# Prompt attention: scores issued ahead of the subtraction for the block two back, absolute values ahead of the weights

## The chip, the cores and the metric

One core of a Trainium2 chip runs the whole program. The metric is the device time of one execution in microseconds; the median of the runs counts. Profiled executions also give a span, from the first to the last recorded instruction.

## The reference, cut to what matters

The program is one inference step of a hybrid decoder layer over a prompt of 1024 tokens and 8 sequences of 8 new tokens. The change lies in one part of it, the stick-breaking attention of the prompt, which has 8 heads of 64 dimensions:

```python
def sb_block(q, k, v, q_pos, k_pos, bias):
    z = (jnp.einsum("bqhd,bkhd->bhqk", q, k).astype(jnp.float32) * (SB_HEAD_DIM ** -0.5)
         + bias.astype(jnp.float32)[None, :, None, None])
    causal = (k_pos[None, :] < q_pos[:, None])[None, None]
    log_stay = jnp.where(causal, jax.nn.log_sigmoid(-z), 0.0)
    log_after = lax.cumsum(log_stay, axis=3, reverse=True) - log_stay
    w = jnp.where(causal, jnp.exp(jax.nn.log_sigmoid(z) + log_after), 0.0)
    return jnp.einsum("bhqk,bkhd->bqhd", w.astype(v.dtype), v)
```

With softplus(z) = log(1 + exp(z)), the weight of a key is exp(z - the sum of softplus over this key and all later keys that the query sees). So the keys have to be gone through from the last to the first, with a running sum carried along.

## The kernel before, in words

The stages run one after the other, with a barrier of all engines between them: the conditioning and input projection, the projection of the linear-attention part together with the attention of the samples, then `stage_prompt_attention` (L1207 to L1457), then the gated linear attention (`stage_gla`), the output projection and the MLP. Only `stage_prompt_attention` is touched.

It works on 4 pairs of heads. For one pair there are 12 blocks, 48 in all, numbered u = 0 to 47. A block is 128 keys against a chunk of up to 512 queries, for both heads of the pair. The list `BLOCKS` (L1213) has eight blocks for the second chunk of queries (keys 7 down to 0) and four for the first chunk (keys 3 down to 0). The first four blocks of either chunk lie on the causal diagonal and are 128, 256, 384 and 512 queries wide; the others are 512 wide. "Block 7 of a pair" below is the last one of the first eight, "block 8" the 128 wide one that follows.

A block goes through five steps, each a function:

- `score` (L1299, TensorE) computes z = q.k (L1308), adds the bias (L1311) and, on the diagonal, the mask (L1317), for both heads, in two banks of PSUM. There are three such pairs of banks (NZ = 3), so score(u) waits until the weights of block u - 3 have been taken (L1306).
- `chain` (L1376, ScalarE) takes the absolute value (L1381), exp(-|z|) (L1384) and ln(1 + .) (L1387), half by half; a half is one head. Blocks up to 256 wide are done with one instruction for both heads (`halves`, L1233).
- `softplus` (L1411, VectorE) adds max(z, 0) (L1416) and splits the sum into a high part (L1421) and a low part (L1423), again by halves.
- `subtract_later` (L1320, TensorE) subtracts from z the sums over the later keys of the block (L1326, L1327) and over the later blocks (L1332), which come from the tile `later`. It waits for the low part of each half (L1325) and for `later` (L1331). `weights` (L1389, ScalarE) then takes exp (L1393), and `multiply` (L1349, TensorE) multiplies with the values (L1359).
- `carry` (L1336, TensorE) adds the block's sums to the running sum in bank C (L1343, L1345); `carry_hi` (L1395, ScalarE) copies it as a rounded high part into `later` (L1400), and `carry_lo` (L1425, VectorE) makes the low part (L1431). The next block's subtraction needs both. `carry`, `carry_hi` and `carry_lo` are left out for the last block of a chunk.

There is no scheduler: each engine has a loop over steps s, and its order is written out by hand.

- TensorE (L1365) in step s: subtract_later(s - 2), carry(s - 2), score(s), multiply(s - 3).
- ScalarE (L1402): weights(s - 2), carry_hi(s - 2), chain(s).
- VectorE (L1448): the output of a finished chunk (L1438, L1440), the first half of softplus(s - 1), carry_lo(s - 2), the second half of softplus(s - 1).

SyncE loads the queries and keys of the pairs (L727), and GpSimd scales them (L736), long before their use.

Of the kernel before, what the change touches and what calls it, by code (L numbers as in the profile page):

```python
# [107 lines left out]
def at_least(eng, sem, value):  # L108

    if not isinstance(value, int) or value > 0:  # L110
        eng.wait_ge(sem, value)
# [1095 lines left out]
def stage_prompt_attention(g, ops):  # L1207
# [10 lines left out]
    TOTAL = NPAIR * NB  # L1218
# [3 lines left out]
    def block_of(u):  # L1222
        c, j = BLOCKS[u % NB]
        return u // NB, c, j

    def left(c, j):
        return max(0, j - c * QB) * P

    def width(u):
        p, c, j = block_of(u)  # L1230
        return 512 - left(c, j)

    def halves(u):  # L1233
        return [slice(0, 2)] if width(u) <= 256 else [slice(0, 1), slice(1, 2)]

    def first(u):
        return u % NB in (0, 8)

    def last(u):
        return u % NB in (7, 11)  # L1240

    def carries_before(u):
        return NCARRY * (u // NB) + CARRY[u % NB]

    def multiplied(u):
        return u + 1

    with ExitStack() as ctx:
# [25 lines left out]
        def z(u, h):  # L1274
            n = 2 * (u % NZ)
            return Z[:, n + h.start:n + h.stop, 0:width(u)]

        def ring(t, depth, u, h):
            return t[:, u % depth, h, 0:width(u)]

        with g.nc.Block() as block:
            @block.sync
            def _(sp):
                ops.load(sp, 0, 0)
                ops.load_values(sp)
                ops.load(sp, 1, 1)
                for p in range(2, NPAIR):
                    sp.wait_ge(s_z, 2 * NB * (p - 1))
                    ops.load(sp, p, p % 2)
# [7 lines left out]
            @block.tensor  # L1297
            def _(pe):
                def score(u):  # L1299
                    p, c, j = block_of(u)  # L1300
                    n, x = width(u), left(c, j)
                    keys, cols = slice(j * P, (j + 1) * P), slice(c * 512 + x, (c + 1) * 512)
                    diagonal = j >= c * QB
                    if u % NB == 0:
                        pe.wait_ge(ops.scaled, p + 1)
                    at_least(pe, s_w, 2 * (u - NZ) + 2)  # L1306
                    for h in range(2):
                        pe.matmul(g.bank[2 * (u % NZ) + h][:, 0:n], ops.k[p % 2][HALF[h], keys], ops.q[p % 2][HALF[h], cols],  # L1308
                                  start=True, stop=False)
                    for h in range(2):  # L1310
                        done = pe.matmul(g.bank[2 * (u % NZ) + h][:, 0:n], ops.bias[HALF[h], 2 * p + h, :], ops.ones[HALF[h], 0:n],  # L1311
                                         start=False, stop=not diagonal)
                        if not diagonal:
                            done.then_inc(s_z, 1)
                    if diagonal:
                        for h in range(2):
                            pe.matmul(g.bank[2 * (u % NZ) + h][:, 0:P], g.ident16[:], g.causal16[:], start=False,  # L1317
                                      stop=True).then_inc(s_z, 1)

                def subtract_later(u):  # L1320
                    p, c, j = block_of(u)
                    n = width(u)
                    for h in range(2):
                        out = g.bank[2 * (u % NZ) + h]
                        pe.wait_ge(s_sl, 2 * u + h + 1)  # L1325
                        pe.matmul(out[:, 0:n], ops.tri[:], sh[:, u % NS, h, 0:n], start=False, stop=False, skip_group_check=True)  # L1326
                        done = pe.matmul(out[:, 0:n], ops.tri[:], sl[:, u % NS, h, 0:n], start=False, stop=first(u),  # L1327
                                         skip_group_check=True)
                        if not first(u):
                            x = left(c, j + 1)  # L1330
                            pe.wait_ge(s_e, carries_before(u))  # L1331
                            done = pe.matmul(out[:, x - left(c, j):n], ops.spread[:, h, :], later[(carries_before(u) - 1) % 2][:, x:512],  # L1332
                                             start=False, stop=True, skip_group_check=True)
                        done.then_inc(s_y, 1)

                def carry(u):  # L1336
                    if last(u):
                        return
                    p, c, j = block_of(u)
                    n, x = width(u), left(c, j)  # L1340
                    at_least(pe, s_e, carries_before(u))
                    for h in range(2):
                        pe.matmul(C[:, x:512], ops.pick[:, h, :], sh[:, u % NS, h, 0:n], start=(first(u) and h == 0), stop=False,  # L1343
                                  skip_group_check=True)
                        done = pe.matmul(C[:, x:512], ops.pick[:, h, :], sl[:, u % NS, h, 0:n], start=False, stop=True,  # L1345
                                         skip_group_check=True)
                    done.then_inc(s_cs, 1)

                def multiply(u):  # L1349
                    p, c, j = block_of(u)  # L1350
                    n, x = width(u), left(c, j)
                    if first(u):
                        at_least(pe, s_ol, 2 * p + 1 - c)
                    pe.wait_ge(s_w, 2 * u + 2)
                    if u == 0:
                        pe.wait_ge(ops.s_v, 32)
                    for h in range(2):
                        head = (2 * p + h) * HD
                        done = pe.matmul(O[HALF[h], x:512], ops.v[:, j, head:head + HD], w[:, u % NW, h, 0:n], start=first(u),  # L1359
                                         stop=last(u), skip_group_check=True)  # L1360
                    done.then_inc(s_pv, 1)

                pe.wait_ge(ops.s_bd, 6)
                pe.wait_ge(ops.s_c, 13)
                for s in range(TOTAL + 3):  # L1365
                    if 0 <= s - 2 < TOTAL:
                        subtract_later(s - 2)
                        carry(s - 2)
                    if s < TOTAL:
                        score(s)  # L1370
                    if s >= 3:
                        multiply(s - 3)

            @block.scalar
            def _(act):
                def chain(u):  # L1376
                    for h in halves(u):
                        n = 2 * u + h.stop
                        at_least(act, s_sl, n - 2 * NA)
                        act.wait_ge(s_z, n)  # L1380
                        act.activation(ring(a_, NA, u, h), z(u, h), ACT.Abs).then_inc(s_abs, h.stop - h.start)  # L1381
                    for h in halves(u):
                        act.wait_ge(s_abs, 2 * u + h.stop)
                        act.activation(ring(a_, NA, u, h), ring(a_, NA, u, h), ACT.Exp, scale=-1.0).then_inc(s_exp, h.stop - h.start)  # L1384
                    for h in halves(u):
                        act.wait_ge(s_exp, 2 * u + h.stop)
                        act.activation(ring(a_, NA, u, h), ring(a_, NA, u, h), ACT.Ln, bias=1.0).then_inc(s_ln, h.stop - h.start)  # L1387

                def weights(u):  # L1389
                    at_least(act, s_pv, multiplied(u - NW))  # L1390
                    for h in halves(u):
                        act.wait_ge(s_y, 2 * u + h.stop)
                        act.activation(ring(w, NW, u, h), z(u, h), ACT.Exp).then_inc(s_w, h.stop - h.start)  # L1393

                def carry_hi(u):  # L1395
                    if last(u):
                        return
                    m, x = carries_before(u), left(*block_of(u)[1:])
                    act.wait_ge(s_cs, m + 1)
                    act.copy(later[m % 2][:, x:512], C[:, x:512]).then_inc(s_eh, 1)  # L1400

                for s in range(TOTAL + 2):  # L1402
                    if s >= 2:
                        weights(s - 2)
                        carry_hi(s - 2)
                    if s < TOTAL:
                        chain(s)

            @block.vector
            def _(dve):  # L1410
# [1351 lines left out]
```

## Time and profile before

| what | value |
|---|---|
| median of 3 runs | 1842.41 us (1842.07 to 1846.49) |
| the profiled execution | 1845.04 us, span 1843.4 us |
| mean granted TensorE clock | 0.945 |
| TensorE matmul busy | 1678.4 us (91%) |
| VectorE busy | 736.4 us (40%) |
| ScalarE busy | 604.0 us (33%) |
| prompt attention, from its first score to its last output | from 519.98 to about 744.5 us of the span |

The profiled execution took 2.63 us more than the median of the runs. In the timeline a row gives the start of an instruction, its duration, its engine, line and operation, and in brackets how long the engine was idle before it and what released it. "x2" is two instructions of a kind merged in one row. The ends of matmuls are modelled, so of TensorE the starts are read rather than the ends. PEclk is the granted clock as a share of 2.4 GHz.

### The profile page before, as it was taken

What the parts mean: (1) busy time and instruction counts of PE and PEld (TensorE: products, weight loads), DVE (VectorE), ACT (ScalarE), POOL (GpSimd) and SP (SyncE); (2) the same over time, 40 slices, a digit from 0 to 9 for tenths busy, and PEclk for the clock granted to TensorE, in tenths of its full rate; (3) what the DMA queues carried; (4) which work ended last, traced back from release to release, by engine and by line L of the source; (5) the groups of instructions that cost most, each with busy time, mean ns of one, the idle gap of its engine ahead of it and who ended that gap; (6) DMA issues with size and microseconds to landing.
All of it is one profiled execution on the core that took longest, in us unless ns stands there. A gap on an engine that the chain in (4) does not pass through costs nothing. (4 is left out here: it accounts for less than half of the span.)

```text
span 1843.4 us, 27703 instructions
## 1 busy us (share of the span) xinstructions
PE 1678.4 (91%) x10864; PEld 1462.3 (79%) x10864; DVE 736.4 (40%) x1252; ACT 604.0 (33%) x1138; POOL 433.8 (24%) x306
## 2 busy tenths in 40 slices
PE   5999996999968888687589899999999999999997
PEld 2899994777744444265479799999999999999997
DVE  3501003444457778446803543232333232323225
ACT  3511102323357778335334431212121211112123
POOL 0022204222200000200144542323333232323230
PEclk8999996999989999577789999999999999999999
DMA  9133117666220000843162221111101111111102
GB/s 326 47 120 125 55 46 234 204 207 195 83 104 23 24 1 1 261 151 107 43 234 92 92 69 47 46 46 35 49 29 46 46 46 46 46 46 46 46 12 98
DMA packets 116177, 164.54 MB, mean 89 GB/s; under 512 B 6970, under 2 KB 80141, under 8 KB 116086
## 3 DMA queue, kind: packets, MB, share of 16 engines
q1 hardware_dynamic: 110864, 146.49, 24.4%
q0 software_dynamic: 5120, 16.78, 2.9%
q8 instruction: 59, 0.97, 0.2%
q14 instruction: 32, 0.26, 0.0%
q10 hardware_dynamic: 102, 0.03, 0.0%
HBM read 141.98 MB, written 21.30 MB: 89 GB/s over the span
## 5 line engine op out<-in xcount | busy, mean ns | idle before, releaser
L468 PE MATMUL psum<-op_hi,out_hi 128*128 128x384 f32 (+1 forms) x960 | 320.7, 334 | 3.7 <-DVEq L2557 2.0
L470 PE MATMUL psum<-op_hi,out_lo 128*128 128x384 f32 (+1 forms) x960 | 314.4, 327 | 0.0
L469 PE MATMUL psum<-op_lo,out_hi 128*128 128x384 f32 (+1 forms) x960 | 314.3, 327 | 0.0
L468 PE MATMUL psum<-mlp_a_hi,out_hi 128*128 128x384 f32 (+1 forms) x768 | 251.0, 327 | 0.5 <-DVE x1T L2584 0.5
L470 PE MATMUL psum<-mlp_a_hi,out_lo 128*128 128x384 f32 (+1 forms) x768 | 250.8, 327 | 0.0
L469 PE MATMUL psum<-mlp_a_lo,out_hi 128*128 128x384 f32 (+1 forms) x768 | 250.5, 326 | 0.0
L2474 POOL TENSOR_TENSOR out_lo<-out_raw,out_hi 128x2048 fp32r<-128x2048 f32 x31 | 143.2, 4621 | 271.6 <-ACT out_hi L2497 271.6
L2570 DVE TENSOR_TENSOR mlp_sq<-mlp_relu 128x384 f32<-128x384 f32 (+1 forms) x96 | 88.3, 921 | 280.4 <-ACT mlp_relu L2512 280.4
L468 PEld LDWEIGHTS psum<-op_hi,out_hi 128*128 128x128 f32 x960 | 181.5, 189 | 7.9 <-DVEq L2557 2.9
L469 PEld LDWEIGHTS psum<-op_lo,out_hi 128*128 128x128 f32 x960 | 181.5, 189 | 2.5
L470 PEld LDWEIGHTS psum<-op_hi,out_lo 128*128 128x128 f32 x960 | 181.3, 189 | 0.0
L2584 DVE SCALAR_TENSOR_TENSOR x1T<-psum,modT,x1T 128x384 f32<-128x384 f32 (+1 forms) x192 | 108.6, 570 | 162.2 <-PE psum L470 155.1
L2497 ACT CAST out_hi<-out_raw 128x2048 fp32r<-128x2048 f32 x31 | 59.1, 1907 | 295.9 <-PE psum L470 295.9
L468 PEld LDWEIGHTS psum<-mlp_a_hi,out_hi 128*128 128x128 f32 x768 | 144.2, 188 | 0.8 <-POOL out_lo L2474 0.8
L470 PEld LDWEIGHTS psum<-mlp_a_hi,out_lo 128*128 128x128 f32 x768 | 144.1, 188 | 0.0
L469 PEld LDWEIGHTS psum<-mlp_a_lo,out_hi 128*128 128x128 f32 x768 | 144.1, 188 | 0.0
L2481 POOL TENSOR_TENSOR mlp_a_lo<-mlp_sq,mlp_a_hi 128x384 fp32r<-128x384 f32 (+1 forms) x96 | 92.8, 974 | 207.9 <-ACT mlp_a_hi L2504 207.9
L2512 ACT ACTIVATE mlp_relu<-psum 128x384 f32<-128x384 f32 (+1 forms) x96 | 45.5, 474 | 266.9 <-PE psum L470 266.9
L468 PE MATMUL psum<-in_hi,op_hi 128*128 128x256 f32 (+1 forms) x288 | 80.7, 280 | 0.0
L470 PE MATMUL psum<-in_hi,op_lo 128*128 128x256 f32 (+1 forms) x288 | 80.4, 279 | 0.0
L469 PE MATMUL psum<-in_lo,op_hi 128*128 128x256 f32 (+1 forms) x288 | 80.3, 279 | 0.0
L468 PE MATMUL psum<-op_hi,in_hi 128*128 128x384 f32 (+1 forms) x216 | 74.6, 346 | 5.4 <-PEq L339 3.2
(338 smaller groups left out, 2999.1 us busy)
## 6 DMA issues: line engine op xcount, KB each, us to landing
sa_k<-in_cache_k SPq DMA_DIRECT2D x64, 256.0 KB, 3.1
sa_v<-in_cache_v POOLq DMA_DIRECT2D x64, 256.0 KB, 3.9
out_raw<-in_w_up SPq DMA_DIRECT2D x16, 1024.0 KB, 5.4
out_raw<-in_w_down SPq DMA_DIRECT2D x16, 1024.0 KB, 4.9
out_raw<-in_w_out SPq DMA_DIRECT2D x12, 1024.0 KB, 4.8
ada_w<-in_w_ada SPq DMA_DIRECT2D x22, 512.0 KB, 4.7
in_raw<-in_w_in SPq DMA_DIRECT2D x8, 1024.0 KB, 6.0
ada_w<-in_w_ada SPq DMA_DIRECT2D x3, 2048.0 KB, 13.8
```

The costliest lines, as they stand in the source:

```text
L468: pe.matmul(out, w_hi, x_hi, start=(k == 0), stop=False)
L469: pe.matmul(out, w_hi, x_lo, start=False, stop=False)
L470: return pe.matmul(out, w_lo, x_hi, start=False, stop=(k == nk - 1))
L2474: pool.tensor_tensor(w.lo[s][:], w.raw[s][:], w.hi[s][:], ALU.subtract).then_inc(w.lo_done, 1)
L2481: pool.tensor_tensor(a_lo[:, m, t0:t0 + tw], q[i % 3][:, 0:tw], a_hi[:, m, t0:t0 + tw], ALU.subtract).then_inc(s_al, 1)
L2497: act.copy(w.hi[s][:], w.raw[s][:]).then_inc(w.hi_done, 1)
L2512: act.activation(r[i % 3][:, 0:tw], g.bank[i % NBANK][:, 0:tw], ACT.Relu).then_inc(s_re, 1)
L2570: dve.tensor_tensor(q[i % 3][:, 0:tw], r[i % 3][:, 0:tw], r[i % 3][:, 0:tw], ALU.mult).then_inc(s_sq, 1)
L2584: dve.scalar_tensor_tensor(out=out, in0=b[:, 0:pw], scalar=g.mod(GA2, kc), in1=out, op0=ALU.mult, op1=ALU.add).then_inc(s_dn, 1)
```

## The change

On TensorE, score(s) moves from behind carry(s - 2) to ahead of subtract_later(s - 2). On ScalarE, `chain` is split: the absolute values of block s (`absolute`) are issued ahead of weights(s - 2), the exponentials and logarithms (`exp_and_log`) stay behind carry_hi(s - 2). Nothing else changes: same instructions, same waits, same buffers, same order on VectorE.

```diff
@@ block.tensor
                 for s in range(TOTAL + 3):
+                    if s < TOTAL:
+                        score(s)
                     if 0 <= s - 2 < TOTAL:
                         subtract_later(s - 2)
                         carry(s - 2)
-                    if s < TOTAL:
-                        score(s)
                     if s >= 3:
                         multiply(s - 3)
@@ block.scalar
-                def chain(u):
+                def absolute(u):
                     for h in halves(u):
                         n = 2 * u + h.stop
                         at_least(act, s_sl, n - 2 * NA)
                         act.wait_ge(s_z, n)
                         act.activation(ring(a_, NA, u, h), z(u, h), ACT.Abs).then_inc(s_abs, h.stop - h.start)
+
+                def exp_and_log(u):
                     for h in halves(u):
                         act.wait_ge(s_abs, 2 * u + h.stop)
                         act.activation(ring(a_, NA, u, h), ring(a_, NA, u, h), ACT.Exp, scale=-1.0).then_inc(s_exp, h.stop - h.start)
...
                 for s in range(TOTAL + 2):
+                    if s < TOTAL:
+                        absolute(s)
                     if s >= 2:
                         weights(s - 2)
                         carry_hi(s - 2)
                     if s < TOTAL:
-                        chain(s)
+                        exp_and_log(s)
```

## Rows read from the trace of the kernel before

**Rows 1.** The page's first line.
```profile
span 1843.4 us, 27703 instructions
```

**Rows 2.** Windows: stretch, its length, busy of each engine, clock, DMA share, GB/s.
```profile
521.00:743.00 222.00, 194.67 (x970) 104.77 (x968) 164.03 (x294) 172.18 (x360) 3.15 (x3) 0.97 0.05 19
...
629.00:683.00 54.00, 47.55 (x246) 25.57 (x244) 41.36 (x76) 43.03 (x91) 0.94 (x1) 1.00 0.00 1
```

**Rows 3.** Waits of 521 to 743 us: who waited for whom, total us, times, longest.
```profile
DVE pa_a L1416 <- ACT pa_a L1387: 45.8, 34, 5.4
ACT pa_a L1381 <- PE psum L1317: 31.7, 26, 14.7
PE psum L1326 <- DVE pa_sl L1423: 27.0, 35, 1.5
...
ACT pa_w L1393 <- PE psum L1332: 14.9, 13, 2.0
ACT pa_a L1381 <- PE psum L1311: 10.4, 15, 0.8
```

**Rows 4.** Timeline among the 512 wide blocks of the second pair, all engines.
```profile
600.67 0.60 ACT L1400 CAST pa_later<-psum 128x512 fp32r<-128x512 f32 x1
...
601.30 0.69 DVE L1431 TENSOR_TENSOR pa_later<-psum,pa_later 64x512 fp32r<-64x512 f32 x1
...
603.21 0.69 DVE L1423 TENSOR_TENSOR pa_sl<-pa_a,pa_sh 128x512 fp32r<-128x512 f32 x1
...
603.96 0.50 PE L1326 MATMUL psum<-pa_sh,pa_negtri 128*128 128x512 f32 x1 [0.27 <-DVE pa_sl L1423]
...
604.77 0.39 PE L1343 MATMUL psum<-pa_sh,pa_pick 128*128 128x512 f32 x1
...
605.78 1.13 PE L1308 MATMUL psum<-pa_q,pa_k 64*128 64x512 f32 x4
605.89 0.60 ACT L1400 CAST pa_later<-psum 128x512 fp32r<-128x512 f32 x1
...
607.08 1.08 PE L1359 MATMUL psum<-pa_w,pa_v 128*64 128x512 f32 x4
607.24 1.09 ACT L1381 ACTIVATE pa_a<-psum 128x512 f32<-128x512 f32 x2 [0.75 <-PE psum L1311]
...
608.09 0.50 PE L1326 MATMUL psum<-pa_sh,pa_negtri 128*128 128x512 f32 x1
...
608.21 1.15 ACT L1384 ACTIVATE pa_a<-pa_a 128x512 f32<-128x512 f32 x2
...
609.25 1.15 ACT L1387 ACTIVATE pa_a<-pa_a 128x512 f32<-128x512 f32 x2
...
611.25 0.60 ACT L1400 CAST pa_later<-psum 128x512 fp32r<-128x512 f32 x1
```

**Rows 5.** Timeline at the narrow blocks: 615 to 619 us, then 631 to 634 us.
```profile
615.44 0.70 PE L1308 MATMUL psum<-pa_q,pa_k 64*128 64x256 f32 x4
615.55 0.60 ACT L1393 ACTIVATE pa_w<-psum 128x512 f32<-128x512 f32 x1 [1.19 <-PE psum L1332]
...
616.59 0.60 ACT L1381 ACTIVATE pa_a<-psum 128x512 f32<-128x512 f32 x1 [0.45 <-PE psum L1317]
617.28 0.63 ACT L1384 ACTIVATE pa_a<-pa_a 128x512 f32<-128x512 f32 x1
...
618.74 0.69 DVE L1416 SCALAR_TENSOR_TENSOR pa_a<-psum,pa_a 128x512 f32<-128x512 f32 x1 [3.01 <-ACT pa_a L1387]
...
631.96 0.60 ACT L1393 ACTIVATE pa_w<-psum 128x512 f32<-128x512 f32 x1 [1.66 <-PE psum L1332]
...
633.70 0.63 ACT L1384 ACTIVATE pa_a<-pa_a 128x512 f32<-128x512 f32 x1
```

**Rows 6.** Timeline at the start of the stage: the absolute values of block 2.
```profile
528.39 0.87 ACT L1381 ACTIVATE pa_a<-psum 128x384 f32<-128x384 f32 x2 [1.85 <-PE psum L1317]
```

**Rows 7.** Timeline behind the stage: the first load of the next stage.
```profile
745.23 0.32 SPq L1586 DMA_DIRECT2D gl_bc<-projT  x1
```

## The prediction

> **What bounds the kernel now.** I went from the page to the windows, then the waits of the stage, then the timeline of single blocks. The page gives a span of 1843.4 us [rows 1]; the stage that is changed fills 222 us of it [rows 2], 12%, so 10 us are 4.5% of the stage. Whatever it saves is the program's: nothing of the next stage starts before the barrier, its first load is issued at 745.23 us [rows 7].
>
> In the windows no engine is full. One steady pair of heads takes 54 us, in which TensorE is busy 47.55, ScalarE 43.03 and VectorE 41.36 us, at a granted clock of 1.00, the 2.4 GHz level [rows 2]. So the stage is bound by chains between the engines, with TensorE next. The waits say the same: VectorE waits 45.8 us for logarithms, ScalarE's absolute values wait 31.7 + 10.4 us for scores (14.7 of it before the stage's first), its weights 14.9 us for subtractions, and TensorE's subtractions 27.0 us for VectorE [rows 3].
>
> The timeline of the 512 wide blocks shows two closed loops [rows 4]. **Loop A, the carried sum:** the copy of the carry starts at 600.67, carry_lo 0.63 later at 601.30, the second half of the next softplus ends at 603.21 + 0.69 = 603.90, its subtraction starts at 603.96, the carry at 604.77, and the next copy at 605.89. That is 5.22 us for one block, with no slack in it. **Loop B, through the score:** from the same 603.90 the subtraction and carry run, then the score at 605.78, the absolute values at 607.24, exp at 608.21, ln at 609.25, weights behind it, and the copy at 611.25. From the copy at 600.67 that is 10.58 us for two blocks, 5.29 each. The second copy came 5.36 us behind the first, because ScalarE was still busy with a chain that had begun late: it had been idle 0.75 us before the absolute values, waiting for the score.
>
> At the narrow blocks the loop through the score is alone [rows 5]. The weights of block 7, second half, start at 615.55. Score of block 9 went out at 615.44, directly behind the subtraction that those weights waited for; absolute values at 616.59, exp at 617.28, and VectorE has been idle 3.01 us when it gets its input at 618.74. The same happens between pairs (weights 631.96, exp 633.70).
>
> **The change, part by part.** No instruction is added or removed: the same matrix products and activations in another order, no DMA moved, no wait added. SyncE's load of a later pair hangs on the count of scores; scores come earlier, so that load can only come earlier.
>
> *Narrow blocks.* After the change score(9) leaves ahead of the subtraction of block 7, and ScalarE has its absolute values done while it waits 1.19 us for that subtraction [rows 5]. Then behind the weights, at 615.55 + 0.60 = 616.15, exp of block 9 can start at once instead of at 617.28: 1.13 us earlier. Between pairs it is 631.96 + 0.60 = 632.56 against 633.70: 1.14. There are four turns of the first kind and three of the second (behind the last block no score follows). I take 7 x 1.13 = 7.9 us. What holds it until the next turn: exp 1.13 us earlier lets VectorE start block 9 earlier, since it is idle 3.01 us there. Late next is the subtraction of block 9: it now has score(11), at least 1.30 us, and the multiplication of block 7, 1.01 us, ahead of it. Walking the starts through with the durations of the rows, it starts some 0.3 us later than today counted from the weights of block 7. That is covered by the absolute values of block 11, 0.97 us, which ScalarE does in that time, and everything from the second half of block 10 on is again 1.1 to 1.3 us early. If that cover were gone, the turn would lose the 0.3. The ends for a turn: nothing (given back behind the score), or up to 1.13 + 0.45, the idle before the absolute values too.
>
> *512 wide blocks.* Loop B is cut: absolute values no longer wait behind a subtraction. Loop A is untouched, 5.22. So blocks go from 5.29 to 5.22, 0.07 on some 16 of them (four steps in each pair): 1.1 us. Three things must fit in 5.22. ScalarE: absolute 0.97, exp 1.04, ln and weights 2.00, copy 0.60, together 4.61 [rows 4]. TensorE: score 1.30 (605.78 to 607.08), multiplication 1.01 (to 608.09), first subtraction 0.81 (as from 603.96 to 604.77), second subtraction and carry 1.82 (603.96 to 605.78), together 4.94. And the order on TensorE: behind a carry, which ends about 0.11 before the copy, come multiplication, score and first subtraction, 3.12, so it is free for the second subtraction 3.01 us after the copy, and its input is ready 603.90 - 600.67 = 3.23 us after it. That leaves 0.22 us spare, the thinnest place of the whole argument. Switches between kinds of matrix product stand in an order that no row shows. I bound each of the three new ones (carry to multiplication, multiplication to score, score to subtraction) by nothing and by 0.3 us, about the 0.27 that TensorE is idle before a subtraction, so 0.9 a block. The nearest rows are a subtraction's three products in 0.81 us and a carry's four with the switch to a score in 1.01: no cost of a switch is seen, and I take none. The other end below: if VectorE's order shifted so that loop A shortened to TensorE's 4.94, another 0.28 x 16 = 4.5 us would go.
>
> The row that bears on order shows a subtraction starting at 603.96, 0.06 us after its input, and a first subtraction at 608.09, directly behind the multiplication [rows 4]: TensorE takes its products one after another. The Trainium skill, page "TensorE: Matmul & The Clock Gate", section "Part 3: Packing small matmuls", says that matmuls start and end strictly in program order. By that rule a subtraction whose input is ready stands behind a whole score, which speaks against this change; the sum has it as 0.3 us, covered, at the narrow blocks and none at the wide ones.
>
> *Start of the stage.* Score(2) no longer waits for the subtraction of block 0. ScalarE is idle 1.85 us there [rows 6]; the next subtraction then comes a slow score later, the clock being still at its lower level. Between 0 and 1.85 I take 1.0, about the middle.
>
> *Sum:* 7.9 + 1.1 + 1.0 = 10.0 us. Against the profiled execution, 1845.04, that is 1835.0; it was 2.63 us above the median, so the median of after is 1842.41 - 10.0 = 1832.4 us.
>
> **The rivals.**
>
> *Given back behind the score.* At each turn a subtraction that is ready waits for a whole score, 1.30 us as in wide blocks, and no absolute values cover it. Then the turns bring less than 1.13 - 1.30, nothing, and 2.1 us remain: 1840.3. For it: ScalarE's weights already wait 14.9 us for subtractions [rows 3], and those get later. Against it: the walk above, where the weights of block 9 are taken no later than ScalarE can come to them.
>
> *The carried sum bounds everywhere.* Loop A also runs through the narrow blocks; if it is the tight one there, earlier scores fill buffers and end nothing sooner. Then only the wide blocks' 1.1 us comes: 1841.3. Against it: VectorE idle for 3.01 us with a logarithm as releaser [rows 5], and block 7 carries nothing.
>
> *Slower: the second subtraction comes too late in wide blocks.* TensorE reaches it after multiplication, score and first subtraction, with 0.22 us spare. If the three new switches cost their upper bound, 0.9 us a block, loop A becomes 0.68 longer on the 24 blocks 512 wide, 16.3 us, against 8.9 saved elsewhere: 1849.8. It decides from 0.22 + 8.9 / 24 = 0.59 us a block. For it: the spare is small, and nothing on TensorE can overtake. Against it: no switch in the rows costs that, and the weights of block s - 3, for which score(s) waits, are done before the copy that precedes it.
>
> **How the numbers follow.** Forecast 0.66; given back 0.12; carried sum 0.12; slower mechanism 0.10. 0.3% is 5.5 us, about what a measurement can tell from no change, so faster starts below 1836.9. The first and last keep their sides save small remains: of the forecast's weight a little falls short of 5.5 us, and of the middle two a little passes it. Faster 0.72, same 0.20, slower 0.08. The range goes from 1832.4 - 4.5, the shorter loop A, to the carried-sum case: 1827.9 to 1841.3; out are the slower case and the tails.
>
> **What would show it.** Right: a steady pair takes about 51.5 us instead of 54 in the windows; a copy of the carry every 5.2 us in wide blocks; exp of blocks 9 and 1 right behind the weights of the last block; the absolute values hardly ever wait for scores, and the stage's end moves from 744.5 to about 734.5. Step by step wrong: subtractions idle for nothing but start later than 0.1 us behind their low parts (given back, or slower); VectorE still idle about 3 us at block 9 (carried sum). The forecast falls if the pair stays above 53 us, or if time changes in another stage.

## The result, and the profile after

The kernel after takes 1831.98 us, median of 5 runs (1827.44 to 1833.39); the kernel before, on the same chip, 1842.07 us (1839.87 to 1846.49). The medians lie 10.1 us apart, which is a ratio of 0.9945. The ratio estimated from all runs is 0.9926, 95% interval 0.991 to 0.9943, and that would be 13.6 us less (10.5 to 16.6). So the change is faster by either, but its size is known to a few us only. The profiled execution took 1832.12 us, span 1830.4 us.

The windows of the kernel after, first the two steady pairs of heads with a stretch of 52 us each, then 10 us of wide blocks. Columns are those of [rows 2].

```profile
574.00:626.00 52.00, 46.69 (x250) 25.53 (x250) 41.62 (x74) 43.49 (x92) 1.05 (x1) 1.00 0.06 21
626.00:678.00 52.00, 47.26 (x256) 25.92 (x253) 41.29 (x75) 43.97 (x93) 0.00 (x0) 1.00 0.00 1
...
590.00:600.00 10.00, 9.55 (x40) 4.63 (x38) 8.19 (x14) 9.08 (x19) 0.00 (x0) 1.00 0.01 2
```

The same work, 47 us of TensorE and 41 of VectorE, now fits in 52 us where it had 54 [rows 2]. The waits of the stage, 521 to 732 us:

```profile
PEld psum L1326 <- DVE pa_sl L1427: 31.7, 34, 1.7
ACT pa_a L1381 <- PE psum L1317: 22.6, 23, 13.3
PE psum L1326 <- DVE pa_sl L1427: 18.8, 28, 1.5
DVE pa_later L1435 <- ACT pa_later L1402: 17.4, 30, 0.8
DVE pa_a L1420 <- ACT pa_a L1389: 17.3, 10, 4.0
...
ACT pa_w L1395 <- PE psum L1332: 14.6, 17, 1.7
```

Against [rows 3]: VectorE's wait for logarithms fell from 45.8 to 17.3 us, the wait of the absolute values for the bias product of wide blocks (10.4 us) is gone, and one wait has grown from 0.5 us in a single place to 17.4 us in 30: carry_lo waits for the copy of the carry. That is the loop of the carried sum, now standing alone. It can be followed in the timeline of the wide blocks of the second pair, all engines:

```profile
594.30 0.59 ACT L1402 CAST pa_later<-psum 128x512 fp32r<-128x512 f32 x1 [0.31 <-PE psum L1345]
...
594.92 0.69 DVE L1435 TENSOR_TENSOR pa_later<-psum,pa_later 64x512 fp32r<-64x512 f32 x1 [0.79 <-ACT pa_later L1402]
...
596.83 0.69 DVE L1427 TENSOR_TENSOR pa_sl<-pa_a,pa_sh 128x512 fp32r<-128x512 f32 x1
...
596.87 1.07 ACT L1381 ACTIVATE pa_a<-psum 128x512 f32<-128x512 f32 x2
...
597.58 0.50 PE L1326 MATMUL psum<-pa_sh,pa_negtri 128*128 128x512 f32 x1
...
598.38 0.39 PE L1343 MATMUL psum<-pa_sh,pa_pick 128*128 128x512 f32 x1
...
599.50 0.59 ACT L1402 CAST pa_later<-psum 128x512 fp32r<-128x512 f32 x1 [0.32 <-PE psum L1345]
```

Copy 594.30, carry_lo 594.92, second half's low part to 597.52, subtraction 597.58, carry 598.38, copy 599.50: 5.20 us, the loop of [rows 4] at its old length. The absolute values start with no idle time before them, where they had waited 0.75 us for the score.

At the turn of the narrow blocks (block 7 to block 9, second pair), the rows that answer to [rows 5], all engines:

```profile
608.74 0.43 DVE L1427 TENSOR_TENSOR pa_sl<-pa_a,pa_sh 128x256 fp32r<-128x256 f32 x1
...
608.87 1.08 PE L1359 MATMUL psum<-pa_w,pa_v 128*64 128x512 f32 x4
608.98 0.60 ACT L1395 ACTIVATE pa_w<-psum 128x512 f32<-128x512 f32 x1 [0.89 <-PE psum L1332]
609.47 0.62 ACT L1386 ACTIVATE pa_a<-pa_a 128x512 f32<-128x512 f32 x1
...
609.88 0.92 PE L1308 MATMUL psum<-pa_q,pa_k 64*128 64x384 f32 x4
...
610.91 0.69 DVE L1420 SCALAR_TENSOR_TENSOR pa_a<-psum,pa_a 128x512 f32<-128x512 f32 x1 [1.74 <-ACT pa_a L1389]
...
610.99 0.31 PE L1326 MATMUL psum<-pa_sh,pa_negtri 128*128 128x128 f32 x1
```

Exp starts 0.49 us behind the start of the weights, where it was 1.73 us in the kernel before; VectorE's idle time there fell from 3.01 to 1.74 us. The rows show the price too: the low part of block 8 is done at 608.74 + 0.43 = 609.17, but its subtraction starts at 610.99, behind the multiplication of block 6 and the whole score of block 10.

To see where the time came from, take the starts of the copies of the carry, 40 in the stage, and their distances in one pair (from the copy of block 10 of the first pair to that of the second, in us, worked out from the timelines):

```
copy of block              0     1     2     3     4     5     6     8     9    10
before                   7.52  3.67  5.19  5.20  5.35  5.22  5.36  7.56  3.88  4.98
after                    7.04  3.85  4.04  4.96  5.19  5.20  5.20  7.55  3.84  3.94
```

Of 3.1 us in this pair 2.2 come at blocks 2 and 10, one block behind the turns, and 0.6 at the wide blocks 3 to 6. Block 8 itself, whose subtraction now stands behind a score, comes no earlier (7.55 against 7.56). In the next pair the gain is 0.65 less, of which the last section tells. Over the stage, from the first score to the first load of the next stage, it is 225.25 us before and 211.87 after, 13.4 less. That is more than the 10.1 of the medians; a second pair of traces, below, shows how far one trace can be off.

### The profile page after: what moved, and what is told of

Its sections match the earlier page's. It is cut to its first block and busy times, and to the rows that moved or that the text cites. A ratio compares the mean times of both kernels' runs of the same rounds, so it can differ in the third digit from the quotient of the medians.

```text
span 1830.4 us, 27703 instructions
## 1 busy us (share of the span) xinstructions
PE 1668.0 (91%) x10864; PEld 1456.9 (80%) x10864; DVE 735.2 (40%) x1252; ACT 604.1 (33%) x1138; POOL 434.3 (24%) x306
```

## The experiments

"The stage" is always the stretch from the first score to the first load of the next stage. The time for a pair is half the distance from the copy of block 10 of the first pair to that of the third, so that neither the stage's start nor its end is in it: 53.93 us before, 51.17 after.

**Only TensorE's part.**

```diff
 # ScalarE, against the kernel after
-                    if s < TOTAL:
-                        absolute(s)
                     if s >= 2:
                         weights(s - 2)
                         carry_hi(s - 2)
                     if s < TOTAL:
+                        absolute(s)
                         exp_and_log(s)
```

> Only TensorE's new order; ScalarE does weights, copy of the carry, absolute, exp, ln as in the kernel before. The stage, from its first score to the first load of the next stage, was 225.25 us before and is 211.87 after. Theory 1 (the gain is the score leaving the loop, and a part of it hangs on ScalarE using its idle time at the turns for the absolute values): wide blocks keep 5.20 us a block, the loop through the score now runs over the copy and the absolute values, 9.9 us for two blocks; at a turn only 1.2 - 0.7 = 0.5 us is gained in place of 1.2. Stage 211.87 + 7 x 0.7 = 216.8, time about 1837. Rival (TensorE's order does it all): stage 212, time 1832.

Measured: ratio to before 0.9954 (0.9937 to 0.9971), 1834.34 us against 1843.98. The stage took 217.09 us, a pair 52.19. Wide blocks lie 5.20 us apart. So the score leaving the loop is enough for the wide blocks, and a part of the gain of the narrow ones is ScalarE using its idle time for the absolute values: theory 1 in kind. The rival, 212, is out. That the stage agrees to 0.3 us is partly luck: of the 5.2 us over the kernel after, 1.9 lie before the first pair's copy of block 3, where TensorE's clock rose 9.9 us behind the first score and not 5.3. Behind the first turn the loss is 1.0 us a pair, 0.5 a turn, where 0.7 was expected, and some 0.2 us of a pair is a collision with GpSimd that this kernel meets twice and the kernel after once (last section).

**Only ScalarE's part.**

```diff
 # TensorE, against the kernel after
-                    if s < TOTAL:
-                        score(s)
                     if 0 <= s - 2 < TOTAL:
                         subtract_later(s - 2)
                         carry(s - 2)
+                    if s < TOTAL:
+                        score(s)
```

> Only ScalarE's new order; TensorE scores behind the carry as before. The absolute values then wait for a score that stands behind the subtraction and carry, and the weights and the copy of the carry stand behind them. Theory 1: the loop of the carried sum gets score and absolute values into it: 3.23 us to the end of the softplus, then 1.88 to the score, 1.46 to the absolute values, 0.97, and weights 0.96: 8.5 us for a wide block in place of 5.3, so about 3.2 x 24 us for the wide and 1 to 2 us for each narrow block: 100 us slower, time about 1940. Rival (ScalarE has idle time enough to take it): under 10 us slower.

Measured: 1976.96 us, one run, 133 us slower. The waits of its stage, 521 to 870 us:

```profile
DVE pa_later L1435 <- ACT pa_later L1402: 141.7, 37, 6.6
ACT pa_a L1381 <- PE psum L1317: 88.5, 30, 5.3
ACT pa_a L1381 <- PE psum L1311: 86.0, 16, 6.4
```

As expected, the absolute values wait for scores, the copy of the carry stands behind them, and carry_lo for the copy. The copies of blocks 3 to 6 lie 7.2 to 11.0 us apart, 9.7 on average, and not 8.5. One reason is TensorE's clock, which now goes back and forth between 1.2 and 2.4 GHz:

```profile
550.00:600.00 50.00, 38.50 (x129) 18.87 (x127) 21.10 (x37) 22.41 (x47) 0.00 (x0) 0.73 0.00 0
```

Block 6 shows what the clock costs: its copy comes 7.24 us behind the one before in the fourth pair, where the granted clock was 1.00 all that time, and 8.37 to 8.77 us in the other three, at 0.80 or 0.81. Whether the loop of 8.5 us is right for the others is not shown.

So the two halves of the change are not additive: TensorE's alone gains 1.7 of the 2.8 us of a pair, ScalarE's alone loses 133 us.

**Only the turns.**

```diff
 # both engines, against the kernel after
+                    early = s % NB in (1, 9)
-                    if s < TOTAL:
+                    if s < TOTAL and early:
                         score(s)
...
+                    if s < TOTAL and not early:
+                        score(s)
```

(On ScalarE the same with `absolute(s)`.)

> The new order on both engines only in the steps that score block 1 and block 9 of a pair; all other steps in the old order. The prediction's term for the seven turns, 7 x 1.13 us, says the stage is 225.25 - 7.9 = 217.3 us, time about 1834 to 1835. Rival (the early exp of block 9 is given back behind a subtraction, and the gain at the narrow blocks comes only together with the early scores of blocks 10 and 11): stage 223 or more, time 1840 to 1842.

Measured: ratio 0.9949 (0.9932 to 0.9966), 1835.28 us. The stage took 216.27 us, 9.0 less than before, where the term of the prediction says 7.9; but a stage's ends differ between executions, so the turns are read from its middle. Behind the copy of block 10 of the first pair there are six more turns; from there to the last copy it is 154.52 us against 161.76, 1.21 us a turn where I took 1.13, or 8.5 for seven. The rival is out: changing eight steps of 48 brings most of the gain. The early scores of blocks 10 and 11 even cost something at first: here, where score 10 stays behind, the copy of block 8 comes 6.33 us behind that of block 6, in the kernel after 7.55. Up to block 10 the two kernels are nearly level (15.25 and 15.34 us from the copy of block 6, 16.42 before).

**Only the narrow blocks.** The same edit with `early = s % NB not in (4, 5, 6, 7)`.

> The new order only in the steps that score the blocks 0 to 3 and 8 to 11 of a pair; the steps that score the 512 wide blocks 4 to 7 in the old order. The wide blocks then keep the loop through the score, 5.29 us a block. Theory 1: stage 211.87 + 16 x 0.09 = 213.3 us, time about 1833.5. Rival (the wide blocks carry a large part): stage over 217 us.

Measured: ratio 0.9946 (0.9929 to 0.9962), 1834.81 us, stage 217.02 us. Of the 3.7 us over what was expected, about 2.0 lie in the last pair, where TensorE's clock fell twice (granted clock 0.83 for 690 to 700 us). Another 2.0 are the wide blocks: the copies of blocks 3 to 6 lie 5.35, 5.22, 5.35 and 5.46 us apart, 21.4 together, against 20.6 in the kernel after. The start of the stage took 1.4 us more, its end 1.3 less. Wide blocks carry 0.8 us a pair against this kernel and 0.6 against before, twice the 0.28 of the prediction, but far from the rival's share.

**The start in the old order.** `early = s != 2`: block 2 of the first pair is scored behind the subtraction, everything else as in the kernel after.

> The kernel after, but step 2, the one that scores block 2 of the first pair, in the old order. In the kernel before TensorE's clock rose at about 530 us, in the one after at about 525, where the early score keeps TensorE busy without a gap. Theory 1 (part of the 3.2 us gained at the stage's start is the earlier clock): the granted clock of 525 to 530 us falls back to 0.5, and the first pair's copy of the carry of block 3 comes 2 to 3 us later than in the kernel after; stage 214 to 215 us. Rival (order alone): the clock rises as early as in the kernel after, and the stage is 1.0 to 1.3 us longer than 211.87.

Measured: the stage took 215.07 us and the copy of block 3 came 22.16 us behind the first score, 18.50 in the kernel after: this trace is as theory 1 says. The windows of the kernel after, then of this one:

```profile
524.00:528.00 4.00, 3.89 (x27) 2.46 (x24) 2.60 (x5) 3.89 (x11) 0.00 (x0) 0.87 0.67 265
```

```profile
524.00:528.00 4.00, 3.15 (x14) 2.63 (x14) 2.72 (x6) 2.10 (x5) 0.00 (x0) 0.50 0.86 334
528.00:532.00 4.00, 4.00 (x16) 1.57 (x13) 0.94 (x3) 2.72 (x7) 1.04 (x1) 0.50 0.02 7
532.00:536.00 4.00, 4.00 (x23) 2.67 (x22) 2.38 (x6) 3.70 (x8) 0.00 (x0) 0.85 0.00 0
```

But the median is 1831.98 us (ratio 0.9927, 0.9909 to 0.9945), the same as the kernel after. One trace for a kernel does not settle a difference in the first 15 us, so both kernels were traced again.

**The kernel after, and the kernel before, once more.**

> The kernel after once more. In its first trace TensorE's clock rose 5.3 us behind the stage's first score, and the stage took 211.87 us; in two runs with the same early score of block 2 it rose 9 to 10 us behind. Theory 1 (when the clock rises differs between executions of one kernel): a stage of 212 to 215 us, according to whether it rises early, with wide blocks at 5.20 and all copies from the second pair on in the same distances as in the first trace. Rival (the order fixes it): 211.9 again. Time 1832.

> The kernel before once more, to see how its stage's start differs between two executions. In its first trace the clock rose 11 us behind the first score, and the stage took 225.25 us. Theory 1: 223 to 226 us, the difference all in the first 20 us; steady pairs 54.0 us. Rival (executions agree): 225.2 within 0.3.

Measured: after again 1832.23 us (ratio 0.9926, 0.9905 to 0.9947, against 1843.62), stage 213.56; before again 1842.73 us in one run, stage 223.19. Cut into three parts, in us, the two traces of either kernel are:

```
first score to copy of block 10, first pair      before 53.76, 53.18     after  49.48,  50.93
from there to the last copy                      before 161.76, 161.78   after 153.15, 153.31
last copy to the first load of the next stage    before  9.73,   8.23    after   9.24,   9.32
```

The middle is the same to 0.2 us in two executions: 8.5 us of gain that both executions have. The ends are not. In the second trace of after the windows show this:

```profile
524.00:528.00 4.00, 4.00 (x20) 2.73 (x16) 2.21 (x5) 3.33 (x9) 0.00 (x0) 0.50 0.72 285
528.00:532.00 4.00, 3.92 (x26) 2.03 (x24) 2.88 (x5) 3.29 (x8) 1.05 (x1) 0.87 0.01 3
```

TensorE's clock went from 1.2 to 2.4 GHz about 9 us behind the first score, 5 in the first trace, with the same instructions and TensorE busy all the time before. To the copy of block 3 it is 19.99 us in this trace and 18.50 in the first; for the kernel before 21.00 and 21.41. So the order gives about 1.0 us there, where the clock rises alike (one trace of each), and the clock would account for the other 1.9 in the first traces. This answers the run with the late start as well: a late clock comes without the old order, so theory 1 is not shown by it.

The stage's end has its share. In the first trace of before the granted clock was 0.57 from 739 to 743 us and the end took 9.73 us; in the second it was 1.00 and the end took 8.23. So most of the 2.1 us between these two traces lies there, and not in the first 20 us as I had expected. The 13.4 us of the first traces were 9.6 in the second; the medians say 10.1 and 11.4.

**How much room TensorE has.** The bias product is issued twice, then four times.

```diff
+                    for h in [0, 1] * 1:          # * 3 in the second kernel
+                        pe.matmul(g.bank[2 * (u % NZ) + h][:, 0:n], ops.bias[HALF[h], 2 * p + h, :], ops.ones[HALF[h], 0:n],
+                                  start=False, stop=False)
                     for h in range(2):
                         done = pe.matmul(g.bank[2 * (u % NZ) + h][:, 0:n], ops.bias[HALF[h], 2 * p + h, :], ops.ones[HALF[h], 0:n],
```

> The kernel after with the bias product of both heads issued twice, so that the bias counts twice. That is some 0.46 us more of TensorE for a wide block ahead of the subtraction. Theory 1 (spare of about 0.22 to 0.3 us at the second subtraction): wide blocks go from 5.20 to about 5.4 us, stage 3 to 6 us longer than 211.87. Rival (the score is well ahead, TensorE has 5.20 - 4.94 us and more to give): wide blocks stay at 5.20.

> The kernel after with the bias product issued four times (the bias counts four times): some 1.38 us more of TensorE for a wide block. Theory 1: beyond the spare every extra microsecond lengthens the block: 5.20 + 1.38 - 0.25 = 6.3 us for a wide block, stage about 211.87 + 24 x 1.1 + 24 x 0.4 = 248 us. Rival: the extra products lie beside the wait for the second half of softplus and cost less than half of it.

Measured: twice, 1834.08 us and a stage of 214.42; four times, 1842.05 us and 224.06 (one run each). My numbers fell twice. The extra product costs less than I took: each head's product uses 64 rows of the array ("64*128" in the rows), and a pair takes 0.23 us, as long as one product of 128 rows, not 0.46. And there is more room. With one pair more the wide blocks stay at 5.20, the rival's number; the stage's 2.6 us are mainly at the first narrow blocks, 0.2 each for blocks 8 and 9 and for 0 and 1. With three pairs more, 0.69 us, the copies of wide blocks lie 5.29, 5.50 and 5.19 us apart. In the 5.50 TensorE has no gap:

```profile
598.68 1.08 PE L1362 MATMUL psum<-pa_w,pa_v 128*64 128x512 f32 x4
599.69 1.13 PE L1308 MATMUL psum<-pa_q,pa_k 64*128 64x512 f32 x4
...
601.68 0.50 PE L1329 MATMUL psum<-pa_sh,pa_negtri 128*128 128x512 f32 x1
...
603.17 0.39 PE L1346 MATMUL psum<-pa_sh,pa_pick 128*128 128x512 f32 x1
...
604.18 1.08 PE L1362 MATMUL psum<-pa_w,pa_v 128*64 128x512 f32 x4
```

From multiplication to multiplication 604.18 - 598.68 = 5.50, less 0.69 of extra products 4.81 us. So TensorE needs 4.81 us for a wide block, and 0.39 is spare, not 0.22: I had added the first product of the second subtraction with the 0.34 us that it shows behind a wait, and without a wait it takes 0.23.

**Shortening the loop of the carried sum.** If it bounds, taking the second subtraction out of it must help.

```diff
 # TensorE; subtract_later and carry cut into halves
-                        subtract_later(s - 2)
-                        carry(s - 2)
+                        subtract_half(s - 2, 0)
+                        carry_half(s - 2, 0)
+                        carry_half(s - 2, 1)
+                        subtract_half(s - 2, 1)
```

> The kernel after, with the carry of each half on TensorE moved: first half's subtraction, first half's carry, then second half's carry, then second half's subtraction. In the loop of the carried sum the second subtraction (0.81 us) and half of the carry (0.46 us) no longer lie between the low part and the copy. Theory 1 (that loop, 5.20 us, bounds the wide blocks): it falls to about 4.0, TensorE's own 4.94 us bounds, so 0.26 us for some 20 blocks: 5 us less, stage 206 to 207, time about 1827. Rival (TensorE or ScalarE bounds the wide blocks already, or weights come later and give it back): stage within 1.5 us of 211.87.

Measured: ratio 0.9935 (0.9917 to 0.9953), 1834.51 us, stage 215.07, wide blocks 5.23: the rival's side, and 3.2 us over the kernel after, more than the rival's 1.5. ScalarE's timeline says why:

```profile
593.81 0.62 ACT L1397 ACTIVATE pa_w<-psum 128x512 f32<-128x512 f32 x1
595.03 0.60 ACT L1397 ACTIVATE pa_w<-psum 128x512 f32<-128x512 f32 x1 [0.61 <-PE psum L1331]
595.53 0.58 ACT L1404 CAST pa_later<-psum 128x512 fp32r<-128x512 f32 x1
```

The copy stands behind the weights of the second half, and those wait 0.61 us for the subtraction that had just been moved back. The loop was opened on TensorE and closed again on ScalarE. So the copy was moved as well:

```diff
 # ScalarE, on top of the kernel above
                     if s >= 2:
-                        weights(s - 2)
+                        weights(s - 2, halves(s - 2)[:-1])
                         carry_hi(s - 2)
+                        weights(s - 2, halves(s - 2)[-1:])
```

> The kernel of the run before (each half's carry ahead of the second subtraction), and on ScalarE the copy of the carry moved ahead of the weights of the second half, where it stood behind them. In that run the wide blocks stayed at 5.23 us: the copy, ready early, stood behind weights that wait for the second subtraction. Theory 1 (the loop of the carried sum bounds, and it had only been closed again over ScalarE): wide blocks fall to TensorE's own time, 5.50 us in the run with four bias products less the 0.69 us of extra products: 4.8 us. 0.4 us for some 16 blocks: stage about 206 to 208, 1827 us. Rival (some other loop stands close below 5.2): wide blocks stay at 5.15 or more, stage 212 or more.

Measured: 1816.54 us, ratio to before 0.9844 (0.9825 to 0.9864), 27 us less than before and 15.7 less than the kernel after in the same comparison. The stage took 200.78 us, a pair 47.48. The copies of blocks 3 to 6 lie 4.25, 4.55, 4.66 and 4.09 us apart: below the 4.8 that I expected, since the block multiplied or scored in the same step is often a narrow one; where both are wide, it is 4.81 from multiplication to multiplication (590.48 to 595.29). The window of its wide blocks:

```profile
585.00:595.00 10.00, 10.00 (x45) 5.46 (x43) 9.37 (x16) 10.00 (x21) 0.00 (x0) 1.00 0.01 2
```

TensorE and ScalarE have no gap left there, where TensorE was busy 9.55 us of 10 after the change. That the carried sum bounded the wide blocks of the kernel after is shown by this; and the narrow blocks gained too (block 10's copy 3.49 us behind block 9's, 3.94 after). That the same loop stood there as well is likely, but no run tells it from others.

## Why the prediction was right

**Time.** 1832.4 was forecast, 1831.98 measured, and 1832.23 the second time; the fall of 10.0 us against 10.1 and 11.4 by the medians (13.6 by the estimated ratio). No step was wrong in kind, but that the sum hits to 0.1 us is luck: the terms below come to 11.8 us as measured, and 0.65 of that went in a collision that the prediction did not have. The sizes, term by term:

- *Turns.* 7.9 us for seven; the run with the turns alone gave 8.5, 1.21 us a turn in place of 1.13. The difference is the handover: I let exp start when the weights ended (0.60), and it started 0.49 us behind their start. The walk behind the turn left out block 8: its subtraction waits behind the score of block 10, and its copy comes no earlier, nor does that of block 9 (3.84 against 3.88 behind that of block 8). From block 10 on, whose copy comes 1.04 us earlier, the walk held.
- *Wide blocks.* 1.1 us from 0.07 a block; it was about 0.14, 0.6 us a pair or 2.3 in all. The loop of the carried sum at 5.20 was right to 0.02. Of the four distances of a pair I had averaged two, 5.22 and 5.36, and left out that the first one, copy to copy into block 3, falls from 5.20 to 4.96. There the copy, carry_lo and the product with `later` are 384 wide: carry_lo starts 0.57 us behind the copy and takes 0.56, in place of 0.62 and 0.69, and the product is 0.06 shorter.
- *Start.* 1.0 us; between traces with the clock rising alike, 1.0. The prediction took it as the middle between nothing and 1.85, so the agreement is luck. The first traces had 2.9 through the clock, which the prediction did not see: it was right for the median more than for its trace. The last output ended at 730.84 us there, not 734.5.
- *Spare on TensorE.* 0.22 us was too small, it is 0.39. It did not enter the sum, but made the slower rival stronger than it was.
- *The pair.* "About 51.5 us" was 51.17.
- *Scores.* "The absolute values hardly ever wait for scores" was too much: behind the first score of the stage 9.3 us of such waits are left of 27.4.

**The rivals.** *Given back behind the score* is there in part: the subtraction of block 8 stands 1.8 us ready behind a multiplication and a score, which takes the turn's gain from blocks 8 and 9, and the gain comes back at block 10, for which ScalarE had already used the time. The run with TensorE's part alone shows what it is worth: with the absolute values not in that gap, a pair takes 52.19 us, 1.0 of the 2.8 lost. *The carried sum bounds everywhere* is true of the wide blocks, whose bound it now is, and yet did not swallow the turns: their gain came, 1.21 us each. *Slower* needed 0.59 us a block of cost from new switches; none appears in the rows: 597.58 for the subtraction is 0.06 us behind its input, as before, and even 0.69 us of real extra work costs 0.1 us on average in a wide block.

The rule of the Trainium skill, page "TensorE: Matmul & The Clock Gate", section "Part 3: Packing small matmuls", that matmuls start and end in program order agrees with these rows: that subtraction of block 8 starts behind the score that stands ahead of it. (Three bias products of the stage are recorded 5 ns ahead of a product of q and k that precedes them in the program.) The rule names the danger of the change rightly; what decides is whether the engine that waits has something else to do.

## What to carry to other kernels

In a pipeline over several engines with orders written by hand, write down each closed loop from rows (start to start, through every engine, with the number of blocks that it spans) and divide; an engine's own work for a block counts as such a loop. The largest quotient bounds, not the busiest engine. A reordering cuts one loop; the next one, 5.22 beside 5.29 us here, tells beforehand how little the steady part can gain, and the gain is where that next loop is absent, here at the turns. And when a link is moved out of a loop on one engine, look for the same link in the order of the next engine: the loop stayed at 5.23 us until the copy was moved past the weights too, and then the program was 15.7 us faster than the kernel after.

## What the runs showed of the hardware

GpSimd and VectorE stood in each other's way. GpSimd scales the queries of the next pair once a pair. In the kernel after, at the third pair's start:

```profile
619.58 1.05 POOL L736 TENSOR_SCALAR pa_q<-pa_q 128x1024 f32<-128x1024 f32 x1 [49.19 <-DMA pa_k<-projT]
619.61 1.55 DVE L1427 TENSOR_TENSOR pa_sl<-pa_a,pa_sh 128x512 fp32r<-128x512 f32 x1
```

The low part, 0.69 us in every other wide block of this trace, took 1.55; it ended 0.53 us behind GpSimd's instruction. The second trace has 1.50, the run with the split carry 1.41. The next copy is 7.69 us behind where other pairs have 7.04 and 7.11: 0.65 us of the stage, lost because the earlier scores moved GpSimd's work onto that instruction. In the kernel before none of the low parts took over 0.694 us. The Trainium skill, page "SBUF — State Buffer", section "🔬 SBUF: two separate sides", says that the two engines share a port pair, which the one that starts first holds for its whole instruction, and that a VectorE operation with two inputs in SBUF needs it against a GpSimd instruction that reads SBUF. The low part is one, and the trace agrees both ways round: in the second pair the low part started first (568.79) and took its 0.69 us, and GpSimd's instruction, 0.13 us behind it, took 1.47 us in place of 1.05.

The time at which TensorE's clock rises at the start of the stage differed between executions: 5 and 9 us behind the first score for the kernel after, 9 and 11 for the kernel before, and about 14 for the fastest kernel, whose stage is short in spite of it. In the kernel after the later rise cost 1.5 us up to the copy of block 3. Together with the clock at the stage's end this makes 1.7 and 2.1 us between two executions of one kernel. Kernels that differ by so much are told apart by distances inside the stage, or by medians, not by one trace.
